# Attention with fp32 value products of two heads on two partition halves, and latent scores in 64-row and 32-row tiles

## The reference, cut to what matters

```python
q = (rmsnorm(q_lat, g_q) @ w_uq).reshape(B, S, 8, 64 + 32)
kv = (rmsnorm(kv_lat, g_kv) @ w_ukv).reshape(B, S, 8, 64 + 64)
k_nope, v = kv[..., :64], kv[..., 64:]
q_pe, k_pe = apply_rope(q[..., 64:], cos, sin), apply_rope(k_rope, cos, sin)  # one k_pe for all heads
s = einsum('bqhd,bkhd->bhqk', qi, k); p = softmax(s); o = einsum('bhqk,bkhd->bqhd', p, v)
# NA: s = where(col_in, q.k + rpb bias, -inf); softmax over 8 rows of 64 keys; o = p v
o = concatenate([o_mla, o_na]) * silu(gate);  out = o @ w_out0
```

## Time and profile before

| | us |
|---|---|
| median of 3 runs | 1789.37 (1789.12 to 1790.64) |
| the profiled execution | 1791.51 |
| its span, first to last instruction | 1789.8 |
| PE busy / DVE busy / ACT busy / POOL busy | 1625.8 / 953.9 / 741.7 / 371.2 |
| granted clock of PE, mean share of full speed | 0.963 |

### The profile page before, as it was taken

The page is one execution under the profiler, slowest core; times in us unless marked ns, Lnnn a source line. Parts: engine busy times, 40 slices in busy tenths (PEclk is TensorE's granted clock), DMA queues, the critical chain, the costliest instruction groups (busy, mean ns, idle before and its releaser), DMA issues. The chain is left out here.

```text
span 1789.8 us, 20445 instructions
## 1 busy us (share of the span) xinstructions
PE 1625.8 (91%) x7578; PEld 1222.2 (68%) x7578; DVE 953.9 (53%) x1669; ACT 741.7 (41%) x1262; POOL 371.2 (21%) x440
## 2 busy tenths in 40 slices
PE   3869999989799998999996999998979999899997
PEld 0457747878566686777874764687856668677786
DVE  2253557863576443676324346885356644467522
ACT  1032447853432334343343235784342243444333
POOL 2001113400010001564100222340111000256410
PEclk9879999999899999999998999999989999999999
DMA  9919600233322252013333940023332225211434
GB/s 339 389 29 204 162 21 1 63 81 96 106 75 68 82 154 80 26 47 109 111 111 96 215 132 21 1 63 86 102 104 72 71 83 155 69 36 36 130 106 142
DMA packets 240962, 182.33 MB, mean 102 GB/s; under 512 B 51342, under 2 KB 220633, under 8 KB 238296
## 3 DMA queue, kind: packets, MB, share of 16 engines
q1 hardware_dynamic: 239832, 178.28, 34.3%
q0 software_dynamic: 1024, 2.67, 0.6%
HBM read 156.71 MB, written 24.21 MB: 101 GB/s over the span
## 5 line engine op out<-in xcount | busy, mean ns | idle before, releaser
L330 DVE TENSOR_TENSOR w_lo<-at,w_hi 128x1024 fp32r<-128x1024 f32 x158 | 207.5, 1313 | 430.9 <-ACT w_hi L323 430.7
L528 PE MATMUL ps<-h_e_hi,w_hi 128*128 128x512 f32 x512 | 206.6, 404 | 16.6 <-DVE h_e_lo L572 13.5
L323 ACT ACTIVATE w_hi<-at 128x1024 fp32r<-128x1024 f32 x158 | 166.2, 1053 | 122.3 <-PE ps L530 118.9
L529 PE MATMUL ps<-h_e_lo,w_hi 128*128 128x512 f32 x512 | 201.7, 394 | 0.0
L530 PE MATMUL ps<-h_e_hi,w_lo 128*128 128x512 f32 x512 | 200.6, 392 | 0.0
L528 PEld LDWEIGHTS ps<-h_e_hi,w_hi 128*128 128x128 f32 x512 | 96.9, 189 | 66.0 <-issue 40.6
L1086 POOL TENSOR_SCALAR at<-at,at 128x512 f32<-128x512 f32 x128 | 87.5, 697 | 175.6 <-DVE at L1011 175.6
L528 PE MATMUL ps<-h_a_hi,w_hi 128*128 128x512 f32 x272 | 109.8, 403 | 12.1 <-ACT at L754 9.0
L530 PEld LDWEIGHTS ps<-h_e_hi,w_lo 128*128 128x128 f32 x512 | 97.0, 190 | 21.3
L529 PEld LDWEIGHTS ps<-h_e_lo,w_hi 128*128 128x128 f32 x512 | 97.1, 190 | 19.6 <-issue 0.5
L529 PE MATMUL ps<-h_a_lo,w_hi 128*128 128x512 f32 x272 | 107.7, 396 | 0.0
(11 more groups left out here) (271 smaller groups left out, 3595.8 us busy)
## 6 DMA issues: line engine op xcount, KB each, us to landing
at<-w_in SPq DMA_DIRECT2D x117, 512.0 KB, 4.2
at<-w_ada SPq DMA_DIRECT2D x16, 1536.0 KB, 14.4
at<-w_out SPq DMA_DIRECT2D x48, 512.0 KB, 4.2
z_kept<-at SPq DMA_DIRECT2D x32, 256.0 KB, 2.3
at<-z_kept SPq DMA_DIRECT2D x32, 256.0 KB, 2.8
at<-rpb_pad SPq DMA_DIRECT2D x32, 224.0 KB, 4.3
t_masked<-at SPq DMA_DIRECT2D x16, 448.0 KB, 4.5
at<-t_masked SPq DMA_DIRECT2D x16, 448.0 KB, 3.3
```

The lines of the kernel that those rows point to most:

```text
L323: act.activation(whi[:, b % PAIRS], wring[:, b % SLOTS], ACT.Copy).then_inc(sem("w_hi"), 1)
L330: dve.tensor_tensor(wlo[:, b % PAIRS], wring[:, b % SLOTS], whi[:, b % PAIRS].bitcast(F32), ALU.subtract)\
L528: pe.matmul(o, stationary[0], moving[0], start=first, stop=False)
L529: pe.matmul(o, stationary[0], moving[1], start=False, stop=False)
```

## The change

Seven things change together, all in layer 0.

1. MLA scores are made for two halves at once, as in NA: heads u and u+1 with the same queries. The 64 plain features of the two heads lie on partitions 0 to 63 and 64 to 127 (`qn`, `kn`), and give four fp32 products over 64 rows. The 32 rotated features follow as four fp32 products over 32 rows, each on its own quarter of the partitions (`qr`, and `kr4`, four copies of the rotated key). PE waits for c_max in place of c_exp.
2. In MLA the maximum is taken by the same two custom instructions as in NA, with a zero bias, and the exponential reads Pt with scale -1.
3. The transposed probabilities and the values stay fp32. ACT copies bank 4 and DVE copies bank 5; the low parts are gone.
4. The values products of two heads are fp32 with 64 columns each and go to partitions 0 to 63 and 64 to 127 of one PSUM bank, every second turn of the loop (`values_of_two`). One copy of 128 partitions on ACT moves two heads to oT.
5. Values come after i-4 in place of i-3. Pt and the transposed probabilities have four buffers.
6. In the second block a pair of heads is copied with one instruction in place of two, the rotated key is copied three times in place of seven, the rotated queries are added in sixteen shorter instructions in place of eight, and the low part of the values is gone.
7. In the first block the low part of the NA values and a wait for the bias table are gone.

```diff
-    vmla = packed("vmla", V0)
+    vmla = by_token(K0 + 4 * T)
     dg = take(T, at=N0 + 20 * T)
-    qcat = chunks(take(8 * T, at=Q0), T)
-    kcat = chunks(take(8 * T, at=K0), T)
+    qn = chunks(take(4 * T, at=Q0), T)
+    kn = chunks(take(4 * T, at=Q0 + 4 * T), T)
+    qr = take(2 * T, at=K0).rearrange("p (n h t) -> p n h t", n=4, t=P)
...
-                nav_low(3)
...
-                    for e in range(2):
-                        act.activation(qcat[0:64, 2 * p + e], b_bank(J_QN + p)[64 * e:64 * e + 64], ACT.Copy, scale=QS)\
-                            .then_inc(sem("b_act"), 1)
+                    act.activation(qn[:, p], b_bank(J_QN + p), ACT.Copy, scale=QS).then_inc(sem("b_act"), 1)
...
-                for m in range(TM):
-                    dve.wait_ge(sem("b_vh"), m + 1)
-                    dve.tensor_tensor(vmla[:, m, :, VD:2 * VD], b_bank(J_V + m).rearrange("p (h d) -> p h d", d=VD),
-                                      vmla[:, m, :, 0:VD].bitcast(F32), ALU.subtract).then_inc(sem("b_v"), 1)
+                    dve.tensor_copy(kn[:, p], b_bank(J_KN + p)).then_inc(sem("b_kn"), 1)
...
-            return attention_pair(j)[1] == 1
+            quad, e = divmod(j, 2)
+            return 2 * (quad // 2) + e, quad % 2
+
+        def ends_two_heads(j):
+
+            u, half = attention_pair(j)
+            return u % 2 == 1 and half == 1
...
-            LT, LV, LO = 2, 3, 4
+            LT, LV, LO = 2, 4, 5
...
-                        pe.wait_ge(sem("c_exp"), j - 1)
+                        pe.wait_ge(sem("c_max"), j)
+                    for m in range(2):
+                        at = (2 * half + m) * P
+                        for e in range(2):
+                            r = 64 * e
+                            pe.matmul(ps(s_bank(j + e) + m), qn[r:r + 64, n, at:at + P], kn[r:r + 64, n],
+                                      start=True, stop=False)
                     for e in range(2):
-                        m = 2 * half + e
-                        last = pe.matmul(ps(s_bank(j) + e), qcat[0:QK, u, m * P:(m + 1) * P], kcat[0:QK, u],
-                                         start=True, stop=True)
-                    last.then_inc(sem("c_s"), 1)
-
-                def score_quad(j):
+                        for m in range(2):
+                            r = 32 * (2 * m + e)
+                            last = pe.matmul(ps(s_bank(j + e) + m), qr[r:r + 32, n, half], kr4[r:r + 32],
+                                             start=False, stop=True)
+                        last.then_inc(sem("c_s"), 1)
+
+                def na_scores(j):
 
                     u, half = attention_pair(j)
                     n = (u - HEADS) // 2
-                    if j == HALVES // 2:
-                        pe.wait_ge(sem("c_exp"), j)
-                    else:
-                        pe.wait_ge(sem("c_max"), j)
+                    pe.wait_ge(sem("c_max"), j)
...
+                def turn(j):
+                    pe.wait_ge(sem("c_nrm"), j + 1)
+                    for q in range(2):
+                        if j >= 1:
+                            pe.wait_ge(sem("c_pd" if q else "c_pa"), j)
...
+                def values_of_two(j):
...
+                    if half == 0 and n >= 2:
+                        pe.wait_ge(sem("c_o"), n - 1)
+                    v = vmla if u < HEADS else nav
+                    pe.wait_ge(sem("c_pa"), j + 1)
+                    for s in range(TM):
+                        if s == 2:
+                            pe.wait_ge(sem("c_pd"), j + 1)
+                        for e in range(2):
+                            last = pe.matmul(ps(6 + n % 2)[64 * e:64 * e + 64, 2 * P * half:2 * P * half + 2 * P],
+                                             v[:, s, (2 * n + e) % HEADS], PT[(j - 1 + e) % 4][:, 2 * P * s:2 * P * s + 2 * P],
+                                             start=(s == 0), stop=(s == TM - 1))
+                            if s == TM - 1:
+                                last.then_inc(sem("c_pv"), 1)
+
...
-                            dve.tensor_reduce(nmx[:, 2 * i:2 * i + 2], ps2(i % 2).rearrange("p (e t) -> p e t", e=2), AX.X,
-                                              ALU.max, negate=True).then_inc(sem("c_max"), 1)
...
+                        h = u - HEADS
+                        if h >= 0 and half == 0:
+                            dve.wait_ge(sem(f"t2_in{h % 2}"), 16 * (h // 2 + 1))
+                        if i >= 4:
+                            dve.wait_ge(sem("c_t"), 2 * (i - 3))
+                        for e in range(2):
+                            at = 6 - 2 * (2 * half + e)
+                            if h >= 0:
                                 bias = T2[:, h % 2].rearrange("p (e k) -> p e k", k=GRID_W)[:, at:at + ROWS, ::-1]
-                                last = dve.tensor_tensor_reduce(chunks(Pt[:, i % 3, e], GRID_W),
-                                                                chunks(ps(s_bank(i) + e), GRID_W), bias, -1.0, 3.0e38,
-                                                                ALU.add, ALU.min, nmx[:, 2 * i + e:2 * i + e + 1])
-                            last.then_inc(sem("c_max"), 1)
-                    if LT <= i < HALVES + LT:
+                            else:
+                                bias = cst("zero").unsqueeze(2).to_broadcast([P, ROWS, GRID_W])
+                            last = dve.tensor_tensor_reduce(chunks(Pt[:, i % 4, e], GRID_W),
+                                                            chunks(ps(s_bank(i) + e), GRID_W), bias, -1.0, 3.0e38,
+                                                            ALU.add, ALU.min, nmx[:, 2 * i + e:2 * i + e + 1])
+                        last.then_inc(sem("c_max"), 1)
+                    if LT <= i:
                         j = i - LT
-                        for q in range(2):
-                            dve.wait_ge(sem("c_hi"), 2 * j + q + 1)
-                            dve.tensor_tensor(PT[j % 2][1][:, q * T:(q + 1) * T], ps(4 + q),
-                                              PT[j % 2][0][:, q * T:(q + 1) * T].bitcast(F32), ALU.subtract)\
-                                .then_inc(sem("c_lo"), 1)
+                        dve.wait_ge(sem("c_t"), 2 * j + 2)
+                        if j >= 4:
+                            dve.wait_ge(sem("c_pv"), j - 3)
+                        dve.tensor_copy(PT[j % 4][:, T:2 * T], ps(5)).then_inc(sem("c_pd"), 1)
...
-                        for q in range(2):
-                            act.wait_ge(sem("c_t"), 2 * j + q + 1)
-                            if j >= 2 and q == 0:
-                                act.wait_ge(sem("c_pv"), j - 1)
-                            act.activation(PT[j % 2][0][:, q * T:(q + 1) * T], ps(4 + q), ACT.Copy).then_inc(sem("c_hi"), 1)
+                        act.wait_ge(sem("c_t"), 2 * j + 1)
+                        if j >= 4:
+                            act.wait_ge(sem("c_pv"), j - 3)
+                        act.activation(PT[j % 4][:, 0:T], ps(4), ACT.Copy).then_inc(sem("c_pa"), 1)
...
-                                last = act.activation(Pt[:, i % 3, e], ps(s_bank(i) + e), ACT.Exp, bias=nmx[:, n:n + 1],
-                                                      accum_out=rsum[:, n:n + 1])
...
+                            last = act.activation(Pt[:, i % 4, e], Pt[:, i % 4, e], ACT.Exp, bias=nmx[:, n:n + 1],
+                                                  scale=-1.0, accum_out=rsum[:, n:n + 1])
```

More of the change, by code:

```diff
@@ L176, in trunk @@
     assert free[0] <= N0
[L177 to L180, removed]
+    Pt = take(8 * T, at=W0).rearrange("p (s u t) -> p s u t", s=4, t=T)
+    T2 = chunks(take(2 * 896, at=W0 + 8 * T), 896)
+    PT = [take(2 * T, at=at) for at in (ring_lo, ring_lo + 2 * T, ring_lo + 4 * T, N0 + 16 * T)]
     assert W0 + 8 * T + 2 * 896 <= N0
@@ L840, in _ @@
                 dve.wait_ge(sem("b_t0"), 1)
[L841 removed]
+                dve.tensor_tensor(kr4[0:32], t0[0:32, 2], t1[0:32, 2], ALU.add).then_inc(sem("b_kpe"), 1)
                 for k in range(2):
@@ L965, in score_quad @@
                                     last.then_inc(sem("c_s"), 1)
+                def turn(j):
[3 more added lines that the diff above has]
+                            pe.wait_ge(sem("c_pd" if q else "c_pa"), j)
+                        for s in (2 * q, 2 * q + 1):
+                            for e in range(2):
+                                at = 2 * P * (s % 2) + P * e
+                                last = pe.transpose(ps(4 + q)[:, at:at + P], Pt[:, j % 4, e, s * P:(s + 1) * P], ident)
+                        last.then_inc(sem("c_t"), 1)
@@ new lines, in values_of_two @@
+                def values_of_two(j):
+                    u, half = attention_pair(j)
+                    n = u // 2
+                    if half == 0 and n >= 2:
[11 more added lines that the diff above has]
+                                last.then_inc(sem("c_pv"), 1)
@@ L967, in _ @@
                 for i in range(HALVES + LV):
```

(21 more changed lines are left out.)

127 lines of the change are left out of this document (31 added, 96 removed).

## The result

The changed kernel takes 1799.56 us in the median of 5 runs (1798.64 to 1803.68); the kernel before, in the same session, 1790.64 (1789.12 to 1792.43). The ratio is 1.0053, with a 95% interval of 1.0040 to 1.0066: slower by 0.5%. The forecast was 1801.0. The span of the profiled execution grew from 1789.8 to 1796.9 us.

A forecast was written before the change was run, and what follows sets the result against it. It took PE as the bound in MLA and the ring in NA; changed, PE would wait for DVE. 2 x (7.7 - 1.2 + 1.2 - 1.2 - 0.7) = 11.6 us more: 1803.1 profiled, 1801.0 median, range 1784 to 1814.

The forecast's parts named there:

- The period of an MLA pair: MLA, steady: TTR to scores 1.37, scores to next TTR 3.09, one ring 3.08; sum 7.54 us, against 7.08 before.
- PE's own path: MLA pair: maximum, DVE's copy, half the transposes, values and shape changes give 7.48 us, almost the same as 7.54.
- Tiles side by side: MLA scores and values: rotated products four at a time, 0.86 us; values' 16 passes two at a time, 1.7 us.
- The cheap-tiles rival: MLA scores: shape change costs nothing, clock stays up; scores to maximum 2.75, period 7.20, total 1791 us; chance 17%.
- NA: NA, steady: two rings set a pair's period, 6.16 us against 6.33 before; 1.2 us less per group.
- the ring: DVE and ACT: maximum, exponentials, reciprocal, next maximum; 3.08 us from one half's TTR pair to the next.
- The blocks before: Ends of the two blocks ahead of attention: 1.2 us less at the first, 0.7 less at the second.
- The start: First MLA scores to first NA scores: 63.6 us against 55.98, 7.7 more per group, with 1.7 added for low clock.
- The row on which the prediction built this: MLA start before the change: clock at half (0.54 in 255.7 to 259.4) after PE had idled 1.68 us.
- The end: Last NA scores to next block: 15.1 us against 14.40, plus 0.5 for the clock; 1.2 more per group.
- The faster rival: Steady pairs: fewer DVE subtractions and four buffers let PE set the period, MLA 6.6, NA about 5.7, 1768 us; chance 12%.

The follow-up runs named there:

- the ring edit: Changed kernel, with DVE in odd turns taking the maximum before the reciprocal of the half before: 1784.59 us, ratio 0.9965.
- PE's order: Changed kernel, with the values products on PE put ahead of the transposes in odd turns: 1791.61 us, ratio 1.0003.
- with the ring opened the kernel before: Kernel before the change, with DVE's reciprocal put behind the next maximum in odd turns: 1791.53 us, ratio 1.0008.
- both orders mended: Changed kernel, in odd turns with the reciprocal behind the next maximum and the values ahead of the transposes: 1770.76 us, ratio 0.9888.
- the runs with filled gaps: Unused fp32 products in each attention block's first gap: five on the changed kernel, 1793.52 us; with both order edits, five 1770.67 us, two 1768.45 us.

## Why the prediction was right, and where it was not

- *The period of an MLA pair* (1.37 + 3.09 + 3.08 = 7.54) held in each part: 1.42 + 3.10 + 3.01 = 7.53. That PE's own path comes out almost the same (7.48) held too: the ring edit leaves 7.52, PE's order 7.47, and only both together free the pair.
- *Tiles side by side.* Values of 16 passes in 1.95, as costed (1.7 and shape changes). The four rotated first passes start at one moment, as one row of the trace shows (lengths in ns, first and last start):

```profile
L934 PE MATMUL ps<-at,at x4: 692/692/692, 287.0 to 287.0; 32*128 32x512 f32 x4
```

  The four second passes start 0.53 after, so eight take 0.86 and the changes of shape about 0.2 more, not 1.1 with the changes of shape on top. The Trainium skill ("TensorE: Matmul & The Clock Gate", Measured speedup vs the span model) gives a gain of 3.07 times for four row tiles. In this trace, for fp32 with 512 columns, the gain in slots alone is 4 times (3.44 us to 0.86); only with the changes of shape counted in (1.07 us) is it 3.2, near the skill's figure.
- *The cheap-tiles rival* fell. The first transposes come 1.07 after the first rotated pass, two slots of 0.43 and about 0.2 more, and the whole step from scores to maximum is 3.10, not 2.75.
- *NA* at 6.16 held for the changed kernel (43.08 over seven intervals), where ring and PE's row both bind. The prediction also took the ring for the bound of NA before, and put the 0.17 us above it down to ACT's copies. That reading failed: with the ring opened the kernel before still takes 6.27 to 6.35 in most pairs, and PE has no gap. So 6.33 was PE's own work with a short wait.
- *The blocks before* held in the first group (-1.98 for -1.9) and gave more in the second (-3.2).
- *The start* was mis-sized and came out right by luck in part. The low clock did not fall into the first group, behind 0.94 us of idle time: the first interval is 7.42, not 9.15. It fell into the second, 10.07 and not 9.24, where it cost 2.6 and not 1.7. Sum 17.49 against 18.39: 0.9 of the 7.7 too many. The row on which the prediction built this, a low clock behind 1.68 us of idle time, is no rule: in the second group of before the same 1.68 us are followed by a granted clock of 1.00 (1099.74 to 1102.74).

```profile
1099.74 3.67 PE L945 MATMUL ps<-at,at 96*128 96x512 f32 x8 [1.68 <-PEq L811]
```

- *The end* was mis-sized the other way. The term of 0.5 for the clock at the last transposes measures 1.6, from the one end that ran at full clock (14.95 and not 16.59): at the low clock the values of the last two pairs took 4.65 and not 3.67, and the transposes 1.74 and not 1.09. Hence +2.2 for +1.2. Without the clock the prediction's end (15.1) was right within 0.2.
- *Outside the stages* the prediction had nothing, and the changed kernel was 3.6 us shorter there, with two stretches of low clock fewer. They don't belong to the change: in the trace of the ring edit they are back (at 705.2 and 742.8). What decides about them stays open. Without these 3.6 us the profiled executions would lie 10.9 apart, nearer to the 11.6 of the forecast. That the stages add up so well is luck in part, since the start was taken too long, the saving in the blocks before too small, and the end too short.
- *The faster rival* named a real possibility and put the wrong condition on it. Fewer instructions on DVE do not open the ring; two changes of order do. With them MLA comes to 6.91 and NA to 5.52 (it said 6.6 and 5.7), and the whole to 1770.76 (it said 1768).

What the change itself is worth: where PE waits for nobody, a pair takes 6.91 in MLA and 5.52 in NA, against 7.08 and 6.27 before. As written, the change makes two other chains longer than that, so it loses 8.9 us; with both orders mended it gains about 20.

## What to carry to other kernels

When a change packs work so that two results come at once, follow both from the moment they are ready: the second one's way through DVE and ACT is now a part of the period, where it used to lie beside the work of the first. Look for two chains of nearly the same length before you judge an edit by its own run: here one order edit gave at most 0.06 us a pair and both gave 0.6. And price the filling and emptying of the pipe apart from the steady period: they held 14 of the 29 us, and by the runs with filled gaps between 5 and 6 of these 14 were clock.

## What the runs showed of the hardware that was not expected

- Order in PE's row sets the overlap of column tiles: 1.95 us for 16 passes in turn, 2.86 with one tile's passes ahead of the other's. In the second case PE still started three of the second tile's passes before the last of the first's.
- Unused products in an idle gap of 4.4 us kept the granted clock of the next group at its upper level, which gave back 2.6 us a group; where the gap was 2.6 us, five of them overran it and gave nothing, and two kept the clock up and let the group start on time (11.96 us to the third group in place of 13.35 to 13.61).
- The idle time just before a group does not alone tell its clock: behind the same 1.68 us the clock was 0.71 over the next 3 us in one group of before and 1.00 in the other, and behind the same 1.92 us the last transposes took 1.09 us once and 1.91 once in one run.
- Taking the maximum before the reciprocal was worth 15 us, though it saves DVE no work; the change had taken 64 us of busy time off DVE, and the kernel was slower.
